# A hybrid streaming encoder layer on one core: the sample attention's rows, bias and first cached keys and values moved under the prompt's attention

## The reference, cut to what matters

```python
# mixer A (band): 8 heads of 64; mixer B (sparse): 8 heads of 64, keys chosen by an indexer
k = concat([k_cache, k_new]); v = concat([v_cache, v_new])   # 512 cached rows + 16 new rows per stream
sc = einsum('bqhd,bkhd->bhqk', q, k) * d ** -0.5
A: sc = sc + rel_bias[clip(distance)]                        # learned relative bias
B: sc = where(selected by the indexer, sc, -inf)
o = einsum('bhqk,bkhd->bqhd', softmax(sc), v)
```

## Time and profile before

| | |
|---|---|
| median of 3 runs | 2784.23 us (2777.97 to 2785.00) |
| the profiled execution's own time | 2785.24 us, with a span of 2783.6 us |
| the prompt's attention | from about 1267 to 1640 us of the span |
| sample loads and turns | from about 1638 to 1655 us |
| sample attention | from about 1655 to 1853 us |
| granted PE clock, mean of the span | 0.973 |

### The profile page before, as it was taken

One profiled execution on the slowest core, in us unless ns is written; L12 is line 12 of the kernel. 1 busy time (PEld: TensorE's weight loads), 2 busy tenths in 40 slices (PEclk: granted clock), 3 DMA queues, 4 the chain that ended last, 5 costly groups with the idle time before them and its releaser, 6 DMA issues. The chain is left out here.

```text
span 2783.6 us, 40367 instructions
## 1 busy us (share of the span) xinstructions
PE 2608.2 (94%) x16684; PEld 2332.9 (84%) x16684; DVE 1355.5 (49%) x2437; ACT 986.1 (35%) x1666; POOL 512.9 (18%) x368
## 2 busy tenths in 40 slices
PE   6999999999999999976998989989899999999997
PEld 6999999988878899974776766657799999998886
DVE  6523232335553698985777723323642323233544
ACT  5332323233432323133666532222433232323332
POOL 0233444100001122821000000000043334410000
PEclk9999999999999999988999989999999999999999
DMA  3122221366622121213000334542112222136553
GB/s 121 48 82 73 84 80 63 121 231 209 226 108 63 65 82 48 97 35 123 24 31 24 122 108 154 178 173 85 46 63 82 72 85 80 63 118 233 194 212 121
DMA packets 153109, 294.28 MB, mean 106 GB/s; under 512 B 14032, under 2 KB 90456, under 8 KB 152928
## 3 DMA queue, kind: packets, MB, share of 16 engines
q1 hardware_dynamic: 146688, 268.12, 28.3%
q0 software_dynamic: 6240, 23.59, 2.3%
HBM read 237.26 MB, written 61.78 MB: 107 GB/s over the span
## 5 line engine op out<-in xcount | busy, mean ns | idle before, releaser
L803 DVE TENSOR_TENSOR f_dl<-f_raw_d,f_dh 128x2048 fp32r<-128x2048 f32 x66 | 151.3, 2293 | 274.6 <-ACT f_dh L619 274.6
L619 ACT ACTIVATE f_dh<-f_raw_d 128x2048 fp32r<-128x2048 f32 x66 | 126.5, 1916 | 322.1 <-PE f_pV L151 292.2
L2082 PEld LDWEIGHTS t_po<-t_v,t_pT 128*128 128x128 f32 x1056 | 134.1, 193 | 34.7 <-DVE t_osb L1806 14.3
L569 ACT ACTIVATE f_gh<-f_pX 128x256 f32<-128x256 f32 x120 | 49.3, 411 | 319.5 <-PE f_pX L151 319.5
L1939 ACT ACTIVATE t_sc<-t_sc,t_small 128x640 f32<-128x640 f32 (+8 forms) x136 | 99.9, 735 | 162.9 <-DVE t_small L1867 128.5
L150 PE MATMUL f_pX<-f_xop,f_u_shi 128*128 128x256 f32 x504 | 149.2, 296 | 0.0
L151 PE MATMUL f_pX<-f_xop,f_u_slo 128*128 128x256 f32 x504 | 149.2, 296 | 0.0
L149 PE MATMUL f_pX<-f_xop,f_u_shi 128*128 128x256 f32 x504 | 149.2, 296 | 0.0
L149 PE MATMUL w_pw<-i_hi,r_T_hi 128*128 128x256 f32 (+1 forms) x504 | 145.2, 288 | 2.6 <-PEq L351 2.6
L150 PE MATMUL w_pw<-i_lo,r_T_hi 128*128 128x256 f32 (+1 forms) x504 | 145.5, 289 | 0.0
L151 PE MATMUL w_pw<-i_hi,r_T_lo 128*128 128x256 f32 (+1 forms) x504 | 144.8, 287 | 0.0
(11 more groups left out here) (372 smaller groups left out, 8138.3 us busy)
## 6 DMA issues: line engine op xcount, KB each, us to landing
f_raw_d<-in_ffn_w_down SPq DMA_DIRECT2D x66, 1024.0 KB, 5.0
hid<-f_gh SPq DMA_DIRECT2D x22, 1152.0 KB, 9.0
f_raw_h<-hid SPq DMA_DIRECT2D x66, 384.0 KB, 5.5
f_g_raw<-in_ffn_w_gate SPq DMA_DIRECT2D x21, 1024.0 KB, 5.3
f_u_raw<-in_ffn_w_up SPq DMA_DIRECT2D x21, 1024.0 KB, 6.4
proj<-w_stage POOLq DMA_DIRECT2D x12, 1152.0 KB, 5.6
i_raw<-in_w_in SPq DMA_DIRECT2D x12, 1024.0 KB, 5.1
f_x<-in_x_prompt SPq DMA_DIRECT2D x16, 512.0 KB, 6.8
```

The costliest lines, as they stand in the source:

```text
L569: act.activation(dst, by_tile(pX[:, c, 0:N[c]]), ACT.Copy).then_inc(s_copy, 1)
L619: act.activation(d_hi[slot(q)][:], raw_d[slot(q)][:], ACT.Copy).then_inc(s_dhi, 1)
L803: dve.tensor_tensor(d_lo[slot(q)][:], raw_d[slot(q)][:], d_hi[slot(q)][:].bitcast(F32), ALU.subtract)
L2082: last = pe.matmul(po[:, h * HD:(h + 1) * HD], pT[:, g % 2, j * P:(j + 1) * P], v[x][:, k0 + j, h * HD:(h + 1) * HD], start=j == 0, stop=j ...
```

## The change

Five `late` steps go into the prompt's list: the bias flip ("sb") after head (1,4,6), and the turning of the sample rows after the heads (1,5,1), (1,5,6), (1,6,6) and (1,7,3). The tiles of the sample loads move: `kc` and `vc` into the places of `kT0` and `v0`, which are free once the first half is done; `srow` (now one mixer at a time), `snT`, `raw_s`, `bias_s` and `rep` into the place of the first half's bias. SP issues the bias, mixer A's sample rows, and keys and values of the items 0 and 1 after `rows_of(11)`, in the second half; mixer B's sample rows follow after the last `rows_of`. ACT spreads the bias in place of DVE. POOL makes `rep` early. `cached_values` is cut in two (`new_values` loads `vn`), and the loop over the items is written anew.

```diff
+LATE_AT = {(1, 4, 6): ("sb", 0), (1, 5, 1): ("sk", 0), (1, 5, 6): ("sq", 0), (1, 6, 6): ("sk", 1), (1, 7, 3): ("sq", 1)}
...
         if h == 2 and n >= 1:
             plan.append(("out",) + tiles[n - 1])
+        if (x, t, h) in LATE_AT:
+            plan.append(("late",) + LATE_AT[x, t, h])
...
-        smp = Plan(nc, tag, at_big)
+        smp = Plan(nc, tag, at_first)
         kc = [smp(f"kc{i}", [P, PAST // P, FW], F32) for i in range(2)]
         vc = [smp(f"vc{i}", [P, PAST // P, FW], F32) for i in range(2)]
+        assert smp.at == rel0
...
-        snT = smp("snT", [P, 2, 2, HT, P], F32)
         late = Plan(nc, tag, at_bias)
-        srow = late("srow", [P, 2, 2, FW], F32)
+        srow = late("srow", [P, 2, FW], F32)
+        snT = late("snT", [P, 2, 2, HT, P], F32)
...
         def _(sp):
...
-            for n in range(2, len(tiles)):
-                rows_of(n)
-
-            for dst, c, r0, r1 in outs:
-                sp.dma_start(dst, proj[r0:r1, c:c + FW]).then_inc(s_out, 16)
-            sp.wait_ge(s_t, units[NH - 1][-1][0] + 1)
-            sp.wait_ge(s_o, NH)
-            for h in range(H):
-                sp.dma_start(raw_s[h * DEC_S:(h + 1) * DEC_S, :],
...
-            for x in range(2):
+            def sample_rows(x):
                 for j in range(2):
...
                 sp.dma_start(vc[s % 2][:], caches[x][1][0, b].rearrange("(k p) h d -> p k (h d)", p=P)).then_inc(s_vc[s % 2], 16)
+
+            def new_values(s):
+                x, b = items[s]
                 r = SEQ + b * DEC_S
                 sp.dma_start(vn[s % 2][:], proj[r:r + DEC_S, x * N_QKV + 2 * FW:x * N_QKV + 3 * FW]).then_inc(s_vc[s % 2], 16)
 
-            cached_keys(0)
-            for s in range(len(items)):
-                if s + 1 < len(items):
-                    cached_keys(s + 1)
+            for n in range(2, len(tiles)):
+                rows_of(n)
+                if n == NP + 3:
+                    sp.wait_ge(s_mx, NP * H)
+                    for h in range(H):
+                        sp.dma_start(raw_s[h * DEC_S:(h + 1) * DEC_S, :],
...
+                    sample_rows(0)
+                    sp.wait_ge(s_o, NP * H)
+                    sp.wait_ge(s_s, NP * H)
+                    for s in range(2):
+                        cached_keys(s)
+                        cached_values(s)
+            sp.wait_ge(s_mf, misc["sq", 0] + 1)
+            sample_rows(1)
+
+            for dst, c, r0, r1 in outs:
+                sp.dma_start(dst, proj[r0:r1, c:c + FW]).then_inc(s_out, 16)
+            sp.wait_ge(s_o, NH)
+            sp.wait_ge(s_s, NH)
+            new_values(0)
+            new_values(1)
+            for s in range(2, len(items)):
+                cached_keys(s)
                 cached_values(s)
+                new_values(s)
             sp.wait_ge(s_out, 16 * len(outs))
...
         def _(pool):
...
-            pool.wait_ge(s_o, NH)
-            pool.wait_ge(s_mf, misc[("o", 1, NP - 1)] + 1)
-            for i in range(2):
-                pool.memset(bd[i][:], 0.0).then_inc(s_zero, 1)
+            pool.wait_ge(s_mx, NP * H)
             pool.memset(rep[:], 0.0).then_inc(s_rep, 1)
...
+            pool.wait_ge(s_o, NH)
+            pool.wait_ge(s_s, NH)
+            for i in range(2):
+                pool.memset(bd[i][:], 0.0).then_inc(s_zero, 1)
...
         def _(dve):
...
-            dve.wait_ge(s_flipped, 3)
-            dve.tensor_copy(bias_s[:, FAR:KS], ps[0][:, 0:KS - FAR]).then_inc(s_be[0], 1)
-            dve.wait_ge(s_be[0], 2)
-            dve.tensor_copy(bias_s[:, 0:FAR], bias_s[:, FAR:FAR + 1].broadcast_to([P, FAR])).then_inc(s_mask, 1)
             dve.wait_ge(s_mask, 2)
...
         def _(act):
...
+                elif e[0] == "late":
+                    m = misc[e[1:]]
+                    act.wait_ge(s_mf, m + 1)
+                    if e[1] == "sb":
+                        act.wait_ge(s_mx, NP * H)
+                        act.activation(bias_s[:, FAR:KS], pm[:, 0:KS - FAR], ACT.Copy).then_inc(s_ma, 1)
+                        act.wait_ge(s_ma, m + 1)
+                        act.activation(bias_s[:, 0:FAR], bias_s[:, FAR:FAR + 1].broadcast_to([P, FAR]), ACT.Copy).then_inc(s_mask, 1)
+                    else:
+                        act.activation(snT[:, e[2], int(e[1] == "sq"), :, :], pm[:].rearrange("p (f c) -> p f c", c=P), ACT.Copy,
+                                       scale=HD ** -0.5 if e[1] == "sq" else 1.0).then_inc(s_ma, 1)
...
         def _(pe):
...
+                elif e[0] == "late":
+                    if e[1] == "sb":
+                        pe.wait_ge(s_bias, 16 * (H + 1))
+                        out = pe_misc(pe, e[1:])
+                        pe.matmul(out[:, 0:KS - FAR], flip_s[:].rearrange("p h q -> p (h q)"), raw_s[:], start=True, stop=True).then_inc(s_mf, 1)
+                    else:
+                        pe.wait_ge(s_sr, 32 * (e[2] + 1))
+                        pe_rows(pe, e[1:], srow[:, int(e[1] == "sq"), :])
...
-            pe.wait_ge(s_bias, 16 * (H + 1))
-            pe.wait_ge(s_mx, NH)
-            pe.matmul(ps[0][:, 0:KS - FAR], flip_s[:].rearrange("p h q -> p (h q)"), raw_s[:], start=True, stop=True).then_inc(s_flipped, 1)
-            pe.wait_ge(s_be[0], 2)
-            pe.wait_ge(s_sr, 64)
-            for x in range(2):
-                for j in range(2):
-                    pe_rows(pe, (("sk", "sq")[j], x), srow[:, x, j, :])
```

More of the change, by code:

```diff
@@ L1575, in attn_phase @@
         flip_s = keep("flip_s", [P, H, DEC_S], F32)
-        at_big = keep.at
         rows = keep("rows", [P, 2, FW], F32)
@@ L1579, in attn_phase @@
         kT, v = [None, None], [None, None]
+        at_first = keep.at
         kT[0], v[0] = keep("kT0", [P, HT, SEQ], F32), keep("v0", [P, NP, FW], F32)
-        rel = Plan(nc, tag, keep.at)
+        rel0 = keep.at
+        rel = Plan(nc, tag, rel0)
         kT[1], v[1] = keep("kT1", [P, HT, SEQ], F32), keep("v1", [P, NP, FW], F32)
@@ L1668, in attn_phase @@
                 order += [(("o",) + e[1:], 1)]
-        order += [((("sk", "sq")[j], x), 0) for x in range(2) for j in range(2)]
+            elif e[0] == "late":
+                order += [(e[1:], 0)]
         order += [(("so", s), 1) for s in range(len(items))]
@@ L1719, in _ @@
             values(1)
-            for n in range(2, len(tiles)):
-                rows_of(n)
-            for dst, c, r0, r1 in outs:
-                sp.dma_start(dst, proj[r0:r1, c:c + FW]).then_inc(s_out, 16)
-            sp.wait_ge(s_t, units[NH - 1][-1][0] + 1)
-            sp.wait_ge(s_o, NH)
-            for h in range(H):
-                sp.dma_start(raw_s[h * DEC_S:(h + 1) * DEC_S, :],
-                             bass.AP(u.tensor, 6 * P * h + FAR + P - DEC_S, [[1, DEC_S], [1, KS - FAR]])).then_inc(s_bias, 16)
-            for x in range(2):
+            def sample_rows(x):
                 for j in range(2):
-                    sp.dma_start(srow[:, x, j, :], proj_v[:, NP, x * N_QKV + (1 - j) * FW:x * N_QKV + (2 - j) * FW]).then_inc(s_sr, 16)
+                    sp.dma_start(srow[:, j, :], proj_v[:, NP, x * N_QKV + (1 - j) * FW:x * N_QKV + (2 - j) * FW]).then_inc(s_sr, 16)
             def cached_keys(s):
@@ L1744, in cached_values @@
                 sp.dma_start(vc[s % 2][:], caches[x][1][0, b].rearrange("(k p) h d -> p k (h d)", p=P)).then_inc(s_vc[s % 2], 16)
+            def new_values(s):
+                x, b = items[s]
                 r = SEQ + b * DEC_S
                 sp.dma_start(vn[s % 2][:], proj[r:r + DEC_S, x * N_QKV + 2 * FW:x * N_QKV + 3 * FW]).then_inc(s_vc[s % 2], 16)
-            cached_keys(0)
-            for s in range(len(items)):
-                if s + 1 < len(items):
-                    cached_keys(s + 1)
+            for n in range(2, len(tiles)):
[4 more added lines that the diff above has]
+                        sp.dma_start(raw_s[h * DEC_S:(h + 1) * DEC_S, :],
+                                     bass.AP(u.tensor, 6 * P * h + FAR + P - DEC_S, [[1, DEC_S], [1, KS - FAR]])).then_inc(s_bias, 16)
+                    sample_rows(0)
[14 more added lines that the diff above has]
+                cached_keys(s)
                 cached_values(s)
+                new_values(s)
             sp.wait_ge(s_out, 16 * len(outs))
@@ L1978, in _ @@
                                    pm[:].rearrange("p (f c) -> p f c", c=P), ACT.Copy).then_inc(s_ma, 1)
-            for x in range(2):
-                for j in range(2):
-                    act.wait_ge(s_mf, misc[(("sk", "sq")[j], x)] + 1)
-                    act.activation(snT[:, x, j, :, :], pm[:].rearrange("p (f c) -> p f c", c=P), ACT.Copy,
-                                   scale=HD ** -0.5 if j else 1.0).then_inc(s_ma, 1)
             act.wait_ge(s_rc, NTT)
```

## The result

The changed kernel takes 2899.64 us (median of 4 runs, 2898.73 to 2904.83), the kernel before 2784.61 us (median of its 4 runs): a ratio over all runs of 1.0423, with a 95% interval of 1.0403 to 1.0443 (the two medians alone give 1.0413). The profiled execution took 2904.83 us with a span of 2903.1 us, 119.5 us more than the span of the old profile; it is the longest of the four, so the trace shows a little more loss than the medians.

What follows compares the result with a forecast made beforehand. PE, busy for 94% of the span, was taken as the bound. 13 x (8.5 + 1.8) = 134 us, less 14.0 at the hand-over, plus 2.2 in the prompt, made +122: 2906 us, range 2880 to 2940.

Steps and rivals of the forecast that it cites:

- The order of SP's loop: Sample attention: load of keys s+1 waits for value s-2, so PE waits 8.5 us, 13 times.
- The clock: Sample attention: after each wait for keys PE resumes at half clock, costing 1.8 us an item.
- the two old waits: Old-run PE waits of 7.18 and 10.08 us; full clock returned 5.6 and 3.2 us after PE resumed.
- The old wait of 5.04 us: Old-run PE wait, read as the clock staying at 1.00 until PE resumed; counted against any clock loss.
- clock held: Rival, sample attention: clock holds through the 13 waits, 13 x 8.5 - 11.8 = +99, 2883 us; chance 0.10.
- the lower end of the range: 2880 us: the clock-held case with the best hand-over (-14.9) and no charge in the prompt.
- The hand-over: Between prompt and sample attention: keys start right after the last output, -14.0 us (bounds -14.9 and -11).
- the prompt: Four turns of sample rows and one bias flip added between PE's heads: +2.2 us, at most 7.5.
- Keys in time: Rival, SP's loop: keys load ahead as before, the 13 waits vanish, -11.8, 2772 us; chance 0.05.
- Clock lost: Rival, sample attention: clock does not return within an item, 13 x 19 - 11.8 = +235, 3019 us; chance 0.06.

Runs made afterwards that it cites:

- The two runs with one loop exchanged: Changed kernel with SP's old order (keys s+1 ahead of values s): 2769.76 us; kernel before with only the new order: 2911.81 us.
- the run with wide matmuls: Changed kernel plus 9 idle 512-column matmuls on PE ahead of the wait for keys 3 to 15: 2880.75 us.
- the run with the keys first: Changed kernel with keys s+1 still held until value s-2 is done, but issued ahead of vc and vn: 2862.67 us.
- the version with the old loop: Changed kernel with SP again asking for keys s+1 ahead of values s: 2769.76 us, ratio 0.9957 to the kernel before.

## Why the prediction was right

The prediction was 2906 us (2880 to 2940); 2899.64 came. Step by step:

**The order of SP's loop** was the step that carried it, and it held as put: the load of keys s+1 stands behind a wait for value s-2, which is PE's last work before these keys. 8.5 us a wait were forecast from the old run's issue at 1696.75 and landing of 7.4 us, 8.55 came, 13 times as counted. The two runs with one loop exchanged show the order to be the cause, with and without the rest of the change.

**The clock** was forecast at 1.8 us an item. In the trace it is 22.09 - 11.88 - 8.55 = 1.66; the run with wide matmuls gives 1.55 by its trace and 1.45 by the medians. The mechanism was right, the size somewhat too high. Read in stretches of 0.5 us, PE worked at half rate for 2.9 to 6.0 us behind the 13 waits, 4.5 on average, and the term had been taken from the longer, 5.6 us, of the two old waits in the earlier trace rows; the other gave 3.2. That is 13 x 0.14 to 13 x 0.35, or 2 to 5 of the 6.4 us by which the forecast was too high. One reading in it was off as well: the 20 transposes in 4.03 us were taken for half clock, but the clock rose among them (to a mean of 0.64 in the old trace from 1656 to 1658). In the item shown 16 take 3.66 us at half clock (1701.17 to 1704.83), 0.23 each and not 0.20.

The old wait of 5.04 us was misread. The clock stood at 1.00 until PE resumed at 838.02, but the next stretch of the old trace is this:

```profile
838.00:840.00 2.00, 1.80 (x8) 1.40 (x8) 0.00 (x0) 0.14 (x1) 0.00 (x0) 0.56 0.00 0
```

So it fell about 0.2 us later, and the eight transposes in the earlier trace rows took 1.80 us where eight take 1.09 at full clock. All three old waits cost the clock; the rival "clock held" and the lower end of the range, which rests on it, had no row on their side. The sentence of the Trainium skill (TensorE: Matmul & The Clock Gate, section HAM oscillation — how this bites in real kernels), that each tile behind a load starts cold, agrees with the traces: the clock was lost behind each of these three waits, behind each of the 13 of the changed kernel, and behind each of the 13 in the run with the keys first, which were only 5.6 us long.

**The hand-over** was forecast at -14.0 us and the prompt at +2.2. Measured in the traces: -15.6, and +2.1 (from the issue of rows_of(11) to the last output's turn it was 1470.70 to 1639.74, it is 1470.62 to 1641.77). Of the extra 1.6 us at the hand-over, 0.9 had been taken off for a low clock, and in this trace the clock stayed at 1.00; it did not do so in every run, as the last section shows. The sum, -13.5, agrees with the 13.4 us that the version with the old loop gained.

**The rivals.** "Clock held" is the run with wide matmuls: 2880.75 where 2883 was worked out. "Keys in time" is the run with the old loop: 2769.76 where 2772 was. "Clock lost" did not occur.

## What to carry to other kernels

A queue that issues loads in order is a dependency of its own: before reordering two loads in it, write down what each waits for and which work the engine that needs them does next. Here a buffer's reuse wait, harmless for the load it guards, was put ahead of a load that was wanted at once, and cost ten times what the early work had gained. Where a moved piece and a rewritten loop come in one change, run them apart.

## What the runs showed that was not expected

Filling a wait with many small PE instructions lengthened the load that PE waited for. This is not a matter of the shape of PE's work. With 70 transposes an item, 12 of 13 groups of loads had a packet of the instruction queue among the data, and their kc landed after 7.9 to 8.8 us; the one group without landed after 7.3. With 9 wide matmuls two groups had such a packet and landed after 8.1 and 8.9 us, the other 11 without it after 7.1 to 7.5. In the changed kernel all 13 were without it, at 7.4 to 7.7. These are the DMA views of two groups of the run with wide matmuls, 1808.67 to 1819.47 and 1788.40 to 1799.20 us:

```profile
q8 instruction: 1, 0.02, 0.8%
...
t_kc<-in_cache_b_k SPq DMA_DIRECT2D x1, 1024.0 KB, 8.9
```

```profile
q1 hardware_dynamic: 1088, 2.13, 56.1%
...
t_kc<-in_cache_b_k SPq DMA_DIRECT2D x1, 1024.0 KB, 7.2
```

Over the whole span the queue moved 132 packets in the changed kernel, 139 with 70 transposes (1820 more instructions in the trace, weight loads among them) and 134 with 9 matmuls (468 more), so one more for some 250 instructions. That fits the fetch of the extra instructions; how one packet holds up the load is not shown.

At the hand-over PE paused for 1.22 us before and after the change alike. In the trace of the changed kernel the clock stayed at 1.00 behind it. In the run with wide matmuls, where PE has the same work up to that point, it fell:

```profile
1636.94 1.11 PE L2055 MATMUL t_pm<-r_ident,t_osb 128*128 128x128 f32 x4 [1.22 <-DVE t_osb L1829]
...
1643.99 3.73 PE L2145 MATMUL t_ps<-t_kTs,t_bd 128*128 128x264 f32 x16
```

```profile
1636.00:1638.00 2.00, 1.06 (x5) 1.06 (x6) 0.69 (x1) 0.00 (x0) 1.69 (x6) 0.61 0.21 37
1638.00:1640.00 2.00, 2.00 (x11) 1.71 (x10) 0.82 (x2) 1.20 (x2) 0.70 (x3) 0.54 0.00 0
```

From the output's turn to the first scores it is 7.05 us there in place of 6.04, so the gain at the hand-over is 14.6 us in one execution and 15.6 in another. Steady work behind a short pause does not by itself keep the clock; what decides it these traces do not show.
